# A decoder trunk with PEER experts on one core: products of dots written to PSUM banks 2 and 3, and V rows issued 16 places behind their U rows

## What is computed

```python
def peer_ffn(hn, w_q, subkeys, u, v):
    ...
    q = (xt @ w_q).reshape(n, PEER_HEADS, 2, PEER_HALF)
    s = jnp.einsum('nhcd,ckd->nhck', q, subkeys)
    s_top, i_top = lax.top_k(s, PEER_TOPK)
    ...
    best, pick = lax.top_k(cand.reshape(...), PEER_TOPK)
    g = jax.nn.softmax(best, axis=-1)
    ...
        u_sel = u[ic]
        v_sel = v[ic]
        act = gelu(einsum('cd,ced->ce', xc, u_sel)) * gc
        return einsum('ce,ced->cd', act, v_sel)
```

## Time and profile before

| | |
|---|---|
| median of 3 runs | 1682.62 us (1680.75 to 1686.96) |
| profiled execution | 1693.95 us, span 1692.1 us |
| granted TensorE clock, mean | 0.955 of full |
| busy: PE, DVE, ACT, POOL | 1401.7, 1065.5, 411.1, 1092.8 us |
| bytes moved by DMA | 628.90 MB, mean 372 GB/s |
| of these indirect (U and V rows) | 553.72 MB, 84.3% of 16 DMA engines' time |

### The profile page before, as it was taken

How to read it: one execution, slowest core, us unless ns; L and a number is a source line. 1 busy time by engine, 2 the same in 40 slices (tenths; PEclk the granted TensorE clock), 3 DMA queues, 4 the chain that set the end, 5 groups by cost and what they waited for, 6 DMA issues and landing times.

```text
span 1692.1 us, 15189 instructions
## 1 busy us (share of the span) xinstructions
PE 1401.7 (83%) x4334; PEld 669.6 (40%) x4334; DVE 1065.5 (63%) x2780; ACT 411.1 (24%) x971; POOL 1092.8 (65%) x1079
## 2 busy tenths in 40 slices
PE   7989889999876779887898688779998687767776
PEld 3445533356422135433464245334564232222222
DVE  4679486675567665785645675787546665566643
ACT  2233232221221232341222222332212111111111
POOL 1038657677766756777776666677766666666664
PEclk9999899999999899998999999989999899998999
DMA  8279989999999999999999999999999999999997
GB/s 305 65 244 373 401 300 375 382 376 404 406 409 409 378 350 405 406 390 396 406 403 406 409 400 404 407 380 371 405 404 410 410 384 356 366 365 371 383 374 280
DMA packets 192130, 628.90 MB, mean 372 GB/s; under 512 B 19448, under 2 KB 23328, under 8 KB 192048
## 3 DMA queue, kind: packets, MB, share of 16 engines
q0 software_dynamic: 152064, 553.72, 84.3%
q1 hardware_dynamic: 39984, 74.22, 12.0%
HBM read 626.81 MB, written 1.05 MB: 371 GB/s over the span
## 4 chain that ended last, share of the span: by engine, by line
PE 33%; DVE 16%; POOL 16%; issue 15%; DMA 11%; another core or an unknown queue 6%; ACT 2%; SPq 0%; DVEq 0%; POOLq 0%; PEldq 0%; ACTq 0%
PE banks L1562 18%; POOL arena L515 16%; DVE arena L1184 8%; DMA arena<-in_peer_v_dram,ids 6%; DMA arena<-in_peer_u_dram,ids 5%; PE banks L1430 4%; PE banks L1261 3%; PE banks L1398 3%; PE banks L1368 1%; PE banks L1209 1%; PE banks L1400 1%; ACT diagonals L788 1%; DVE ndex_scores_and_softplus L1034 0%; PE banks L1421 0%
## 5 line engine op out<-in xcount | busy, mean ns | idle before, releaser
L1562 PE MATMUL banks<-arena,diagonals 128*128 128x512 f32 (+1 forms) x2096 | 1009.8, 619 | 195.6 <-DMA arena<-in_peer_v_dram,ids 87.7
L515 POOL DMA_INDIRECT arena<-in_peer_v_dram,ids x528 | 542.7, 1028 | 313.7 <-issue 133.3
L515 POOL DMA_INDIRECT arena<-in_peer_u_dram,ids x528 | 545.6, 1033 | 271.9 <-issue 157.9
L1562 PEld LDWEIGHTS banks<-arena,diagonals 128*128 128x128 f32 (+1 forms) x2096 | 379.6, 194 | 743.2 <-issue 680.2
L1184 DVE SCALAR_TENSOR_TENSOR arena<-arena,banks 128x1024 f32<-128x1024 f32 x260 | 317.0, 1219 | 199.9 <-DMA arena<-in_peer_u_dram,ids 126.1
L1184 DVE SCALAR_TENSOR_TENSOR arena<-arena,x_rows 128x1024 f32<-128x1024 f32 x268 | 327.2, 1221 | 133.5 <-DMA arena<-in_peer_u_dram,ids 104.0
L788 ACT ACTIVATE diagonals<-ident,activations 128x128 f32<-128x128 f32 x512 | 156.4, 388 | 288.2 <-issue 119.0
L1430 PEld LDWEIGHTS banks<-x_norm_T,weight_blocks 128*128 128x128 f32 x960 | 123.1, 197 | 39.0 <-issue 28.7
L1430 PE MATMUL banks<-x_norm_T,weight_blocks 128*128 128x128 f32 (+1 forms) x960 | 125.4, 285 | 11.6 <-DVE x_norm_T L859 5.9
L770 ACT ACTIVATE gelu<-dots 128x8 f32<-128x8 f32 x66 | 13.7, 208 | 377.5 <-DVE arena L1184 225.7
L1398 PE MATMUL banks<-weight_blocks,heads_T 128*128 128x512 f32 x128 | 62.1, 601 | 0.1
(11 more groups left out here) (242 smaller groups left out, 895.4 us busy)
## 6 DMA issues: line engine op xcount, KB each, us to landing
weight_blocks<-in_peer_w_q_dram SPq DMA_DIRECT2D x64, 512.0 KB
arena<-in_peer_u_dram,ids POOLq DMA_INDIRECT x528
arena<-in_peer_v_dram,ids POOLq DMA_INDIRECT x528
weight_blocks<-in_a_w_o_dram SPq DMA_DIRECT2D x16, 512.0 KB
weight_blocks<-in_b_w_q_dram SPq DMA_DIRECT2D x16, 512.0 KB
weight_blocks<-in_b_w_o_dram SPq DMA_DIRECT2D x16, 512.0 KB
arena<-in_a_w_in_dram SPq DMA_DIRECT2D x6, 1024.0 KB, 13.5
weight_blocks<-in_kv_w_dram SPq DMA_DIRECT2D x8, 512.0 KB
```

What stands on the lines that cost most here:

```text
L515: pool.indirect_dma_start(out=ring[:, slot, :], out_offset=None, in_=table, in_offset=bass.IndirectOffsetOnAxis(ap=ids[:, k:k + 1], axis=0 ...
L1562: ins = mm(bank[:w, 6 + m, :], DG[:, k, :w], ring[:, slot, 512 * m:512 * m + 512], start=first, stop=k == (14 if n == NG - 1 else 15) and ...
```

## The change

Two things change together.

1. **Products to banks 2 and 3.** In parts of the seven windows with x in banks 0 and 1, a dot writes its product to banks 2 and 3 (`YP`) in place of the slot. `PRODUCTS` gives for each window the last dot that does so: 110 to 127, 131 to 143, 147 to 165, 263 to 271, 275 to 293, 391 to 399 and 403 to 527. By the order of DVE these are 212 dots (the change speaks of 235). Three windows' first dots also wait until the projections have left the banks (`s_ev`), and PE's first `kv` block of layer 1's tiles waits for the dots up to 165 and 293.
2. **LAG 16.** V rows and their sums run 16 places behind. `V_AT` says which V rows belong to a place; at places 480, 488 and 496 two are issued and summed, so that the last are 13 behind. `fin` moves from place k = 14 of the group behind a tile to k = 1 of the one after, and the norms at the start of `attention_b` move by one place.

```diff
-LAG = 13
+LAG = 16
+CATCH_UP = (480, 488, 496)
...
+        V_AT, _v = {}, 0
+        for _s in range(16 * NG + LAG):
+            _to = min(_s - LAG + 1 + sum(_s >= a for a in CATCH_UP), 16 * NG)
+            V_AT[_s] = [divmod(v, 16) for v in range(_v, _to)]
+            _v = max(_v, _to)
...
+        PRODUCTS = ((127, (0, 2, "pq", 2)), (143, None), (165, None), (271, (1, 1, "pq", 2)), (293, None),
+                    (399, (1, 2, "pq", 2)), (527, None))
+        YP = bank[:, 2:4, :].rearrange("p b n -> p (b n)")
...
-            return ((norm_work(18, "b", 0) if i == 1 else []) + norm_work(20 if i == 1 else 19, "b", i) +
+            return ((norm_work(18, "b", 0) if i == 1 else []) + norm_work(21 if i == 1 else 20, "b", i) +
...
-                if s >= LAG:
-                    v_rows_of((s - LAG) // 16, (s - LAG) % 16)
+                for n, k in V_AT[s]:
+                    v_rows_of(n, k)
...
+                    product = ring[:, slot, :]
...
                         if first == 16 * n + k:
                             dve.wait_ge(s_xp, w + 1)
+                            if PRODUCTS[w][1]:
+                                dve.wait_ge(s_ev, EVENTS[PRODUCTS[w][1]] + 1)
...
+                        if first <= 16 * n + k <= PRODUCTS[w][0]:
+                            product = YP
...
-                    stt(ring[:, slot, :], ring[:, slot, :], 1.0, x_row, ALU.mult, ALU.mult,
+                    stt(product, ring[:, slot, :], 1.0, x_row, ALU.mult, ALU.mult,
...
-                    if k == 14 and n - 1 in ENDS:
-                        fin(n - 1)
+                    if k == 1 and n - 2 in ENDS:
+                        fin(n - 2)
...
+                    pe.wait_ge(s_dots, PRODUCTS[2 if i == 1 else 4][0] + 1)
                     two_banks(e)
...
-                if s >= LAG:
-                    v_sum((s - LAG) // 16, (s - LAG) % 16)
+                for n, k in V_AT[s]:
+                    v_sum(n, k)
```

## The result

The changed kernel takes 1689.12 us (median of 20 runs, 1681.89 to 1694.51), the kernel before beside it 1682.97 (20 runs). The ratio is **1.0039, 95% interval 1.0021 to 1.0056**: 6 us slower, where the prediction said 2 us faster. It lies in the range given, and still within 0.5%, but the sign is wrong. The profiled execution has a span of 1687.0 us, that of before 1692.1: one profile of each has the order of the medians reversed. So a step of this size can be read from medians, and in the profiles only where all of them agree.

The account below looks back on a forecast made before the run. The prediction took the kernel to be bound by row traffic, with traffic missed in some stretches. Its terms 0 + 3.8 - 3 - 3, about -2 us, carried over to the median gave 1680 us, range 1650 to 1705.

Parts of the forecast that it names:

- case A: Whole kernel as summed, neither late sums nor gather length holding the queue: 1680 us, alone 1674 to 1691, chance 0.40.
- The product's place: Dots on DVE writing products to banks 2 and 3: taken 0 per dot, bounds -134 to +1219 ns.
- The waits that come with it: `s_ev` before three dots and PE's wait before `kv`: cost 0, without cover at most 5 us, twice.
- B: Late windows: products written to SBUF make results late, removing them gives 1646, half of it 1664; chance 0.25.
- D: Bank-to-bank dots are slow and decide above 1.64 us once DVE fills the stretch: about +40, 1720; chance 0.12.
- The start, +3.8: Three V rows fewer moved at the start, paid at places 480, 488, 496: +3.8 us, bounds 0 to +5.9.
- PE, -3: PE has done three sums fewer at a given place, so attention work comes earlier: -3 us, between 0 and -5.9.
- the diagonals, -3: V sums waiting for diagonals get three more places, PE's 15.8 us of waits go: -3 us, between 0 and -15.8.
- C: POOL's waits on PE shrink because three more places mean diagonals are never late: up to 15.8 us, 1667; chance 0.13.
- E: The shift costs more: deferred rows (+5.9) and ACT's diagonals waiting for late sums, +10 to +15, 1695; chance 0.10.
- `fin` and norms: Both move with the V sums: 0, at most 2.6 us for each of two norms.

Follow-up runs that it names:

- e1: Changed kernel with only the products in banks 2 and 3, V rows back to 13 behind, fin and norms as before: 1680.45 us, 0.998 of before.
- e11: Repeat, in another comparison, of the changed kernel with products in banks alone and V rows 13 behind: 1684.41 us, 1.0022 of before.
- e16: Third run of the changed kernel with products in banks alone and V rows 13 behind: 1644.73 us, 1.0001 of before.
- e15: The whole changed kernel again, in a comparison whose traces lack the late news: 1644.92 us, 1.0006 of before.
- e5: Changed kernel with products in banks, V rows starting 16 behind but caught up at places 64, 72, 80, fin and norms as before: 1696.48 us, 1.0006.
- e13: Repeat: changed kernel, products in banks, start 16 behind, caught up at places 64, 72, 80, fin and norms as before: 1648.57 us, 1.0016.
- e18: Kernel before with POOL's first V gathers 11 places behind, V gathers skipped at places 104 and 112, PE's sums 13 behind: 1689.8 us, 0.9983.
- e14: Changed kernel, V rows starting 13 behind, skipped at places 64, 72, 80, then 16 behind with fin and norms as in the change: 1647.81 us, 1.0013.
- e6: Changed kernel with products in banks, V rows 13 behind, only the second layer's norms one group later: 1693.25 us, 0.9989 of before.
- e4: Changed kernel with the catch-up at places 64, 72, 80 instead of 480, 488, 496, fin left where 16 places need it: 1703.49 us, 1.013.
- e9: The whole changed kernel again, in a second comparison: 1689.7 us, 1.0054 of before.
- e12: Repeat of the changed kernel with the 16 places alone, all products written to their slots: 1689.87 us, 1.0039 of before.
- e8: Changed kernel with the catch-up at places 525, 526, 527 instead of 480, 488, 496: 1695.21 us, 1.0 of before.
- e3: Changed kernel without the catch-up, so the last V rows are 16 behind: 1684.17 us, 1.0012 of before.
- e10: Repeat of the changed kernel with the catch-up at places 525, 526, 527: 1688.47 us, 1.0032 of before.

## Why the prediction was wrong

The time lies inside the 1674 to 1691 of case A, and most of A's other signs came: gathers of 940 ns, 37.8 us of POOL's waits, 376 GB/s. That the number is close owes much to terms that are all small. The sum was about -2 us, and the measured change is +6.1, clear of zero, so the mechanism as summed is wrong.

- **The product's place.** Taken 0 by the dots that read a bank. Measured: +67 ns a dot, near the low end of the bounds of -134 to +1219, and hidden as argued (e1, e11 and e16: 0.998, 1.0022, 1.0001). What was left out is the accumulator's read, an instruction of its own with 58 of the 67 ns. The waits that come with it showed nothing.
- **B, late results because of the product in SBUF.** Refuted: POOL loses 37.8 us in 1350 to 1650 as before, at 376 GB/s, with all 106 products of the stretch in banks. Its ground was also not quite so: in the trace of before, 11 of POOL's 32 waits put down to "remote" and 3 of DVE's 32 (18.5 and 12.3 us) lie in stretches where x comes from SBUF. The Trainium skill, "SBUF — State Buffer", section "SBUF: two separate sides", has VectorE and GpSimd lock each other out only for two-port modes and two SBUF inputs of VectorE, and a dot with x in a bank has one; the trace agrees that the product's place does not matter to the gathers (938 and 937 ns). e15 and e16 show besides that the late news is no property of the kernel: on another occasion it was absent with either placement.
- **D, a slow dot.** 1228 ns is far from the 1.64 us at which it decides.
- **The start, +3.8.** The term's size is within what was measured, but the term isn't shown at the end of the kernel: V row 0 went out 5.9 us later and the 65th gather 4 us later in the mean, while by 160 us one row was missing and not three, e5 and e13 with the late start alone gave 1.0006 and 1.0016, and the gain of e18 is not clear of zero. Its bounds were 0 to +5.9.
- **PE, -3, and the diagonals, -3: the steps that failed.** Both were booked for engines that the queue does not wait for. e14 has the 16 places in the middle without the late start: it lacks the +3.8 and should show both gains, and it took 3.1 us more than e16 by the medians (1.0013 and 1.0001, both without late news). PE's wait for diagonals was 7.0 us where before has 15.8, but e1 has 4.9 with 13 places, so most of the 15.8 was not a price of the 13 places. What stops POOL in the late stretch is the news of a sum that was done long before, which the prediction itself had found; a V sum that starts earlier does not make its news earlier. I priced -6 us from a row of waits and three sums' time, without showing for either one V slot that had run out by it. No run shows a gain from either term. Without these two terms the sum is +3.8, or 1686.4 us as the prediction carries it over; measured were 1689.1, and +6.1 between the medians.
- **C, fewer POOL waits for PE.** Refuted by the same rows: 21.2 us for PE in 1350 to 1650 against 16.0.
- **E.** It had the right sign, at +10 to +15 where 6 came. Its half on the start is discussed above. Its other half, ACT's diagonals waiting for sums, has a row of 48.0 us in eight waits, where before has 7.5 in one; but before has 67.7 us of unknown releaser at the same place, and e1 has 45.1 us in six waits for PE with 13 places, so this can't be called a cost of the three places.
- **`fin` and norms** at 0: e6 agrees for the norms; e4 shows what `fin` costs when it does not move with the sums.
- **Still open:** which step of part 2 costs the 6 us, since neither half costs them alone (e5, e13, e14) and the start's 4 us at the 65th gather could be followed no further; why the cost is there in the comparisons of the change, e1 to e4 and e9 to e12, and not in e8 or e15; whether the three double places cost something where they stand (e3, e8 and e10 give 1.0012, 1.0, 1.0032); and why the whole change cost 1.0006 where its two halves cost 1.0016 and 1.0013. What makes the news late on some occasions was not tried.

The one kernel that may beat both is e18, POOL's first V gathers 11 places behind on the kernel before: 0.9983, with an interval that reaches no change; it was run once.

## What to carry to other kernels

In a kernel bound by its traffic, rows put off while the queue is not full may have to be paid for later, and slack given to engines that the queue did not wait for returned nothing here: before booking a gain from a wait, follow it to a slot that ran out, and look whether the wait is as long in a second profile (15.8 us in one, 4.9 in another with the same 13 places). Gathers can be moved apart from the work that uses them, but only as far as their slots are really free. And a schedule edit worth 0.4% must be repeated in several comparisons, each against its own runs of before: here one edit measured 1.0039, 1.0054 and 1.0006.

## What the runs showed of the hardware that I had not expected

- A dot of 128 x 1024 whose unused product goes to a bank takes 1228 ns against 1219, but reading its accumulator takes 141 ns against 83: the destination of the big output slows the small instruction behind it.
- The late news of semaphores comes and goes on one and the same chip. With it (all comparisons but one) the kernel before took 1682 to 1695 us and POOL had 36 to 71 us of "remote" waits in every profile of it and its variants; without it (e13 to e16) 1645.85 us, no such wait, and 409 GB/s to the end. The two go together with 2.2 to 3% of the time, more than any edit here, e4 included. In the trace of before, the wait of POOL that ends at 1507.80 ends 0.25 us after a wait of 3.84 us of DVE (line 1136, put down to "remote" too, ended at 1507.55): one cause may hold up both, which no run tested.
- The granted clock goes with it: 0.955 to 0.967 in the profiled executions with late news, 0.978 to 0.981 in those without. Which follows from which is not shown.
